# Gate multiplied per pass and prompt rows scattered into the output, in place of a last phase over all rows

## What is computed

```python
def run_block(args):
    tok, e = args
    gu = h[tok] @ w1[e] + b1[e]
    gate, up = jnp.minimum(gu[:, :D_FF], 7.0), jnp.clip(gu[:, D_FF:], -7.0, 7.0)
    act = (up + 1) * (gate * jax.nn.sigmoid(1.702 * gate))
    return act @ w2[e] + b2[e]
...
out = out * buf_g[:, None]                    # the router's gate of each (row, expert)
y = jnp.zeros_like(h).at[buf_t].add(out)      # four experts' results added per row
...
return x + gate_ffn[:, None, :] * y           # x: the row after attention; gate_ffn: one vector
                                              # for the prompt, one per sample row
```

## Time and profile before

| | |
|---|---|
| median of 3 runs | 1370.66 us (1370.13 to 1372.12) |
| profiled execution, its own time | 1364.26 us |
| its span | 1362.6 us |
| PE busy | 1216.6 us, 89% |
| DVE busy | 666.8 us, 49% |
| ACT busy | 489.4 us, 36% |
| POOL busy | 215.3 us, 16% |
| bytes moved | 481.25 MB, mean 353 GB/s |
| scatters into yd | 31 from ost, 4 from gu |

### The profile page before, as it was taken

The page is one execution under the profiler, slowest core; times in us unless marked ns, Lnnn a source line. Parts: engine busy times, 40 slices in busy tenths (PEclk is TensorE's granted clock), DMA queues, the critical chain, the costliest instruction groups (busy, mean ns, idle before and its releaser), DMA issues.

```text
span 1362.6 us, 17470 instructions
## 1 busy us (share of the span) xinstructions
PE 1216.6 (89%) x6463; PEld 722.7 (53%) x6463; DVE 666.8 (49%) x970; ACT 489.4 (36%) x703; POOL 215.3 (16%) x285
## 2 busy tenths in 40 slices
PE   4899899969999979998999789998789999999871
PEld 2454455543675646764754266654466654747330
DVE  3532663473785664444863134354335354847303
ACT  5121432222564433334643123343223343736210
POOL 2312320030111211103111111021111021111001
PEclk9799899979999989999999899999889999999786
DMA  9940985399999999999999999999999999999995
GB/s 333 378 118 6 317 285 200 130 355 373 405 392 376 404 407 382 406 404 368 412 404 404 404 387 386 370 382 405 403 392 373 358 385 411 407 409 405 412 390 190
DMA packets 113562, 481.25 MB, mean 353 GB/s; under 512 B 12473, under 2 KB 13800, under 8 KB 83706
## 3 DMA queue, kind: packets, MB, share of 16 engines
q1 hardware_dynamic: 100346, 451.44, 83.7%
q0 software_dynamic: 12768, 27.47, 7.5%
q10 hardware_dynamic: 362, 1.19, 0.3%
HBM read 463.46 MB, written 24.14 MB: 358 GB/s over the span
## 4 chain that ended last, share of the span: by engine, by line
PE 54%; DMA 12%; SPq 5%; DVE 5%; issue 1%; ACT 1%; POOLq 0%; ACTq 0%
PE bank L2316 51%; DMA raw<-in_w 9%; SPq L536 3%; DVE rawr L2155 2%; DMA yd<-ost,slot_tok 1%; SPq L546 1%; PE bank L2363 1%; DMA yd<-gu,slot_tok 1%; PE bank L2340 1%; SPq L542 1%; ACT hi L1984 1%; DVE gu L2119 1%; DVE gu L2117 0%; DMA yf<-yd 0%; DVE yf L2306 0%
## 5 line engine op out<-in xcount | busy, mean ns | idle before, releaser
L2155 DVE TENSOR_TENSOR rawr<-raw,hi 128x1024 fp32r<-128x1024 f32 x288 | 341.3, 1221 | 130.3 <-ACT hi L1984 127.2
L1984 ACT CAST hi<-raw 128x1024 fp32r<-128x1024 f32 x288 | 295.1, 1049 | 157.2 <-PE bank L2316 116.4
L2316 PE MATMUL bank<-raw,xT_even 128*64 128x512 f32 (+1 forms) x704 | 138.5, 616 | 4.7 <-DMA raw<-in_w 4.6
L2316 PE MATMUL bank<-raw,aT 128*32 128x256 f32 (+1 forms) x992 | 109.6, 456 | 15.1 <-DMA raw<-in_w 15.0
L1876 POOL DMA_INDIRECT yd<-ost,slot_tok x31 | 54.4, 1755 | 364.1 <-ACT ost L1967 364.1
L2316 PE MATMUL bank<-raw,xT_odd 128*32 128x512 f32 (+1 forms) x544 | 87.6, 670 | 14.7 <-DMA raw<-in_w 14.6
L2316 PE MATMUL bank<-hi,aTh 128*128 128x512 f32 x240 | 78.9, 411 | 18.2 <-DVE rawr L2155 18.2
L2316 PE MATMUL bank<-hi,xTh_even 128*128 128x512 f32 x256 | 84.6, 413 | 5.5 <-DVE rawr L2155 5.5
L2117 DVE TENSOR_SCALAR gu<-bank 128x512 f32<-128x512 f32 (+1 forms) x50 | 31.4, 628 | 103.3 <-PE bank L2316 103.3
L2316 PE MATMUL bank<-rawr,xTh_even 128*128 128x512 f32 x256 | 81.1, 399 | 0.0
L2316 PE MATMUL bank<-hi,xTl_even 128*128 128x512 f32 x256 | 80.8, 398 | 0.0
(11 more groups left out here) (373 smaller groups left out, 1668.5 us busy)
## 6 DMA issues: line engine op xcount, KB each, us to landing
raw<-in_w SPq DMA_DIRECT2D x356, 1024.0 KB, 18.0
raw<-in_w SPq DMA_DIRECT2D x48, 512.0 KB, 11.9
raw<-in_w_ada SPq DMA_DIRECT2D x21, 1024.0 KB, 7.1
w_in_sb<-in_w_in SPq DMA_DIRECT2D x4, 1280.0 KB, 17.0
w_out_sb<-in_w_out SPq DMA_DIRECT2D x4, 1024.0 KB, 9.3
early<-in_w SPq DMA_DIRECT2D x4, 1024.0 KB, 12.3
ada_more<-in_w_ada SPq DMA_DIRECT2D x3, 1024.0 KB, 13.8
xs<-in_x_prompt SPq DMA_DIRECT2D x4, 512.0 KB, 12.8
```

What stands on the lines that cost most here:

```text
L1984: nc.scalar.copy(m.hi[:, (2 * n + h) % HI, :], m.raw[:, slot, h * D:(h + 1) * D]).then_inc(hi_done, 1)
L2155: v.tensor_tensor(m.rawr[slot][:, half], m.raw[:, slot, half], m.hi[:, (2 * n + h) % HI, :].bitcast(F32), ALU.subtract).then_inc(lo_done, 1)
L2316: return nc.tensor.matmul(out, lhsT, rhs, start=start, stop=stop, skip_group_check=True)
```

## The change

The last phase over the prompt's rows is gone. yd is gone too: in its place is `sums`, a DRAM table of eight rows for the samples, zeroed by one DMA. x already lies in y_prompt, and each block's rows are now multiplied by gate_ffn and added there.

- DVE makes a second index per block, `slot_sample` (two small operations in `slots`): the row number in `sums` for sample rows, out of bounds for prompt rows.
- When a block is evacuated, POOL first scatters it, unmultiplied, into sums (`scatter_samples`, 35 indirect DMAs more, each waiting for the one before).
- DVE then waits for that to land and multiplies the block in place by gf (`scale`; the last pass goes to another part of gu and waits only for the evacuation). `scale(p - 2)` stands in DVE's program of pass p behind the rows' indices and ahead of `low_x`.
- POOL scatters the multiplied block with addition into y_prompt, where the sample rows are out of bounds; in its loop this stands behind `gather(p + 2)`. `scat_done` now counts these.
- gf is loaded early in the passes. At the end SP loads the eight sums, DVE multiplies and adds the samples' x, and SP stores them.
- To make room, one of the three bias buffers moves to another place, and xf, yf and their semaphores go.

The core of the diff:

```diff
@@ experts: sync @@
+                if n == RING + 2:
+                    sp.dma_start(m.gf[:], m.modd[3, NS:NS + 1, :].to_broadcast([P, D])).then_inc(gf_in, 16)
...
             sp.wait_ge(unit_used, extra * UNITS + ALL_USED)
-            sp.wait_ge(summed, 1)
-            for t in range(TP):
-                sp.dma_start(m.yf[:, t, :], m.yd[tok(t), :]).then_inc(y_in[t], 16)
-            sp.dma_start(m.yfs[:], by_64(m.yd[tok(TP), :])).then_inc(y_in[TP], 16)
-            for t in range(TP):
-                if t == 1:
-                    sp.wait_ge(f_added, 1)
-                else:
-                    sp.wait_ge(f_ready, max(t, 1))
-                sp.dma_start(y_rows(o, t), m.yf[:, t, :]).then_inc(f_out, 16)
-            sp.wait_ge(f_ready, TP)
+            sp.wait_ge(scat_sample, extra * 16 + 16 * BB[NE])
+            sp.dma_start(m.yfs[:], by_64(m.sums)).then_inc(sums_in, 16)
+            sp.wait_ge(f_ready, 1)
+            sp.wait_ge(scat_done, extra * 16 + 16 * BB[NE])
             sp.dma_start(by_64(y_rows(o, TP)), m.yfs[:]).then_inc(f_out, 16)
@@ experts: gpsimd @@
+            def scatter_samples(p):
+
+                n = ROWS_PER[ORDER[p]]
+                gp.wait_ge(sample_ready, p + 1)
+                for b in range(blocks(ORDER[p])):
+                    k = BB[p] + b
+                    gp.wait_ge(out_ev, k + 1)
+                    if k:
+                        gp.wait_ge(scat_sample, 16 * k)
+                    gp.indirect_dma_start(sums_of[n],
+                                          bass.IndirectOffsetOnAxis(ap=m.slot_sample[:, p % 6, b:b + 1], axis=0),
+                                          out_rows(p, b), None, bounds_check=sums_limit[n], oob_is_err=False,
+                                          compute_op=ALU.add).then_inc(scat_sample, 16)
+
             def scatter(p):
...
-                    gp.wait_ge(out_ev, k + 1)
+                    gp.wait_ge(scaled, k + 1)
                     if k:
                         gp.wait_ge(scat_done, 16 * k)
-                    gp.indirect_dma_start(yd_of[n],
+                    else:
+                        gp.wait_ge(m.x1_out, 3 * 16)
+                        gp.wait_ge(m.x1_last, 2 * 16)
+                    gp.indirect_dma_start(y_of[n],
                                           bass.IndirectOffsetOnAxis(ap=m.slot_tok[:, p % 6, b:b + 1], axis=0),
-                                          out_rows(p, b), None, bounds_check=limit[n], oob_is_err=False,
+                                          scaled_rows(p, b), None, bounds_check=y_limit[n], oob_is_err=False,
                                           compute_op=ALU.add).then_inc(scat_done, 16)
...
                 if p >= 2:
-                    scatter(p - 2)
+                    scatter_samples(p - 2)
                 pick_static(p + 4)
                 gather(p + 2)
+                if p >= 2:
+                    scatter(p - 2)
@@ experts: vector @@
+                v.tensor_scalar(m.sample_row[:, 0:b], m.slot_raw[:, 0:b], float(n),
+                                m.offs[:, 3 + n // 2:4 + n // 2], ALU.mult, ALU.add).then_inc(sample_step, 1)
+                v.wait_ge(sample_step, count)
+                v.scalar_tensor_tensor(m.slot_sample[:, buf, 0:b], m.sample_row[:, 0:b], -64.0, m.sample_row[:, 0:b],
+                                       ALU.mult, ALU.max).then_inc(sample_ready, 1)
+
+            def scale(p):
+
+                if p < 0:
+                    return
+                n, w = ROWS_PER[ORDER[p]], D // ROWS_PER[ORDER[p]]
+                if not p:
+                    v.wait_ge(gf_in, 16)
+                for b in range(blocks(ORDER[p])):
+                    if p < NE - 1:
+                        v.wait_ge(scat_sample, 16 * (BB[p] + b + 1))
+                    else:
+                        v.wait_ge(out_ev, BB[p] + b + 1)
+                    for q in range(n):
+                        part = slice(P // n * q, P // n * q + P // n)
+                        last = v.tensor_tensor(scaled_rows(p, b)[part], out_rows(p, b)[part],
+                                               m.gf[part, w * q:w * q + w], ALU.mult)
+                    last.then_inc(scaled, 1)
...
                 last_act(p - 1, 1)
+                scale(p - 2)
                 low_to(USED[p, 4] + 1)
...
             last_act(NE - 1, 1)
+            scale(NE - 2)
+            scale(NE - 1)
```

94 lines of the change are left out of this document (52 added, 42 removed).

## The result

The changed kernel is slower: **1379.17 us** (1377.09 to 1379.97, 5 runs) beside 1371.68 us for the kernel before in the same comparison, ratio 1.0071 (95% interval 1.0055 to 1.0088), 7.5 us. A second comparison gave 1377.92 beside 1366.66 us, ratio 1.0063 (1.0038 to 1.0088). The prediction was 1365.0: wrong in sign. The result lies inside its range, but the upper part of that range came from the rivals and not from the forecast's own working.

What follows compares the result with a forecast made beforehand. PE sets the pace in two-block (A) passes, the weight stream afterwards; no matmul runs in the tail. Terms -13.2 + 0.5 + 1 + 5 + 0 + 1 = -5.7 us on the median 1370.66 gave 1365.0 us, range 1356.5 to 1383.

Steps and rivals of the forecast that it cites:

- the cover: In the passes: queued weight loads and DVE's idle time would absorb delays, so holds behind A passes cost 0.
- Tail, -13.2: After the last matmul: the final phase over the prompt's rows goes, and the span ends 13.2 us sooner.
- the case that the prediction priced at 13.9: At the end: if pass 30's prompt scatter landed in 5.1 us, the samples' side would bind; gain 13.9 us.
- Two small DVE operations, +0.5: Sample-row indices each pass; in pass 0 they lie ahead of everything: +0.5 us.
- Packets, +5, bounds 0 and 29: In the passes: 35 more indirect DMAs take DMA time, 7 us in the body, +5 us charged; bounds 0 and 29.
- The rival's 24 us: Rival, slower by small packets: 35 scatters cost 24 us by the skill's estimate, total 1384; 1389 at upper bound; chance 0.08.
- Multiplications, +1: In the passes: 35 blocks multiplied on DVE, 43 us, mostly covered by its idle time: +1 us.
- Hold before pass 8, +1: Before pass 8: DVE held about 2.5 us in a stretch that runs into PE's: +1 us.
- Nobody waits long: In one-block passes: results come on average 32 us apart, so the longer-held result tile delays nobody for long.
- Hold behind A passes, 0: Behind two-block passes 8, 16, 22: PE resumes 9.4 us later, absorbed by queued weights: 0; uncovered, up to 28 us.
- slower, by the hold: Rival, behind A passes: serial sample scatters hold DVE, then PE, then the weight ring; 1379 half, 1393 all; chance 0.17.
- two conditions: For that hold to show: landings from 11.3 us on, or PE's lower clock and its delay reaching the next A pass.

Runs made afterwards that it cites:

- r3: Changed kernel with earlier multiplication and scatters (early pairs): both scatters read the multiplied block, neither waits for the other; 1359.70 us, ratio 0.9935.
- e9: r3 plus a second sample scatter per block, from gf into another table, that nothing on ACT, DVE or PE waits for; 1362.05 us, ratio 0.9938.
- e3: Changed kernel with one column of each piece multiplied in place of all, for passes 0 to 30; 1367.60 us, ratio 0.9999.
- e10: r3 with one column multiplied in place of all, for passes 0 to 30; 1357.91 us, ratio 0.9929.
- the square: Late then early place: scatters serial (upper row), changed kernel 1.0063, e8 1.0148; scatters in pairs (lower row), r2 1.0017, r3 0.9935.
- e2: Changed kernel with sample scatters of passes 0 to 30 reading gf, and DVE not waiting for them to land; 1368.01 us, ratio 1.0011.
- e6: Changed kernel with DVE's waits for sample scatters removed in all passes but the two-block (A) ones and the last; 1371.99 us, ratio 1.0040.
- b1: Kernel before, with ACT's wait behind a two-block (A) pass shortened to the first block's scatter; 1368.47 us, ratio 0.9988.
- r5: r3 with ACT's wait behind a two-block (A) pass shortened to the first block's scatter; 1359.05 us, ratio 0.9924.
- e5: Changed kernel with DVE's waits for sample scatters removed in the three two-block (A) passes only; 1375.42 us, ratio 1.0048.
- e7: Changed kernel with ACT's wait behind a two-block (A) pass shortened to the first block's scatter; 1376.88 us, ratio 1.0053.
- r2: r3 with DVE's multiplication back behind the indices and POOL's pair of scatters behind the gather; 1370.24 us, ratio 1.0017.
- e8: Changed kernel, scatters still serial, with multiplication moved ahead of the indices and both scatters ahead of the gather; 1386.10 us, ratio 1.0148.
- e4: Changed kernel without sample scatters of passes 0 to 30, multiplication moved ahead of the indices, POOL's scatter ahead of the gather; 1356.56 us, ratio 0.9933.

## Why the prediction was wrong

**The step that failed is the cover.** The prediction wrote down the chain behind an A pass and its length correctly, and then charged nothing for it ("I take 0"), 1 us for the like hold before pass 8 and 1 us for the multiplications, because the weight queue and DVE's idle time would take them up. Its terms for the passes come to 7.5 us (0.5 + 1 + 5 + 0 + 1); the passes lost 22 to 24.

- **Tail, -13.2:** right; -14.9 measured. Pass 30's prompt scatter landed in 4.2 us and the samples' side came last (their store left at 1375.16, right behind the addition of 1374.85), which is the case that the prediction priced at 13.9.
- **Two small DVE operations, +0.5:** open. The first indices came 1.7 us later, but at 286.2 to 294.0 in the other kernels, whose heads hardly differ.
- **Packets, +5, bounds 0 and 29:** too high by most of it. The DMA time of each, 0.1 to 0.2 us, was near rows 7; that it would be paid was wrong, 34 more cost 0.4 us, give or take 4. The rival's 24 us are excluded too. They came from the Trainium skill, "DMA: Bandwidth & Descriptors", section Bandwidth, which has 0.68 us of DMA time for a transfer of 4 KB. The traces of r3 and e9 don't agree with that figure for these scatters, sent beside the weights' packets: they have 0.1 to 0.2 us for each.
- **Multiplications, +1:** mis-sized. In the changed kernel they are worth 9 to 10 us by their length alone (e3); only in the early pairs is it the 1 us or so of the forecast (e10, not told from 0 nor from 4). The reason given, "the cover is its idle time", overlooked where that time lies. DVE's 15 us of idle time behind an A pass lie ahead of the look-up, and the change put the multiplication behind it and POOL's prompt scatter behind the gather. The prediction noted that DVE reaches the multiplication at 889.9, 5.5 us after the scatter's old start, and charged nothing. This place, both moves together, costs 11 us in the pairs' row of the square.
- **Hold before pass 8, +1:** mis-sized. The changed kernel is 15.5 us behind by index 11, of which e2 and e6 give some 4 to 7 us to the waits for sample scatters. "Nobody waits long" was argued from results 32 us apart on average. What counts is who stands behind the waiting instruction, and in a B pass that is PE's next group of transposes (3.72 us at 529.10). The rest of the 15.5 is open: r3, without those waits, has 7.9 us there.
- **Hold behind A passes, 0:** the mechanism was right, and the 9.4 us about right (12.8, 9.1, 9.7 in the three stretches), and in part the cover: 9.3 and 3.3 us came back between them. But each delay was set against the whole depth of the queue as if it came alone. Here the 15.5 us ahead of pass 8 and two late waits per A pass used it together, and the depth itself shrank, from 18.0 to 13.4 us for the median load. This reading is argued from b1 and r5, where the hold behind pass 8 taken alone was worth nothing in the end, and from the loads; the queue's depth itself was not varied.
- **The rival** "slower, by the hold" (0.17; 1379 for half of it) gave the time that came, in part by luck. Of its two conditions the first, landings of 11.3 us and more, did not come about: behind pass 16 they took 6.2 and 8.7 us. The second, a lower clock after the pause and a delay that reaches the next A pass, did. Its 14 us are the three holds alone, where the passes lost 22 to 24. Taking the waits of DVE away behind A passes (e5) or shortening ACT's (e7) did not bring the time back, so as the one cause it fell too.

Together, by the ratios of the second comparison: 8.6 us slower with 14.9 gained in the tail are 23.5 us in the passes. On the way from the changed kernel over r2 to r3, 6.3 go with the serial wait (left column of the square, which also moves POOL's scatter of the samples behind the gather), 11.2 with the place (lower row), each give or take 4, and 6.0 are still in r3 (14.9 - 8.9). The split holds for this way only: over e8 the early place first makes the kernel 11.6 us slower, and taking out the wait then gives 29.1. The last 6 us stay open. e4 has no sample scatters and the same ratio, but its tail is 14.3 us and r3's 12.5, so its passes lose some 2 us less; e10 gives at most part of the rest to the multiplication. That each prompt scatter still leaves later than its old one, by a multiplication and a handover from DVE to POOL, was not tested apart.

## What to carry to other kernels

A step put into a filled program costs by its place in each engine's order at least as much as by its length: here the same multiplications, and the scatters that follow them, cost 11 us behind a wait in whose idle time they fit. A new wait for a DMA belongs where nothing urgent is queued behind it; better is to remove the dependence, here by scattering the multiplied block twice at once and putting the samples' own factor in at the end as a ratio (which asks that no gate_ffn of the prompt is zero). And a queue's depth has to be held against the sum of the delays in a stretch and not against each alone; this last is the reading that fits here, not one that a run varied.

## What was not expected of the hardware

Behind its pause of 6.98 us PE's group of four transposes took 1.09 us (923.66), the group ahead of it 0.66 us (914.16); the mean granted clock of 905 to 945 was 0.91 of 2.4 GHz, where it was 1.00 before, and from 923 to 930 it was 0.72. The 16 matmuls behind those transposes took 4.71 us (924.68), the 16 of the same kind behind before's second transposes 3.65 (896.02), at a clock of 1.00. The sample scatters cost POOL more than the DMA engines: its busy time rose by 67.5 us, of which some 60 us are the 35 scatters (31 from ost take 53.3 us), and no term of the sum had it. That e9's 34 more of them, with 57.4 us more of POOL (337.7 in place of 280.3), changed the time by 0.4 us, give or take 4, fits with their falling into POOL's idle time in that kernel.
